# Turning the new query and key vectors at the end of an attention step, and splitting them one step later

## What is computed

```
h = rms_norm(x) ;  q, k, v, gates = split(h @ w_in)
q, k = rms_norm of each head's 64 columns
y_a = block-sparse attention (8 heads) ;  y_b = three-branch attention (8 heads)
x = x + (sigmoid(g_a) * (y_a @ w_br_moba) + sigmoid(g_b) * (y_b @ w_br_nsa)) @ w_o
u = causal conv3(rms_norm(x) @ w_up) ;  x = x + (gelu(u_a) * u_b) @ w_down
x = x + sigmoid(x @ w_ple_gate) * (p @ w_ple)
```

## The kernel before

| steps | vectors turned | beside them on PE |
|---|---|---|
| 4-7, 12-15, 20-23 | units 2, 3, 4 | projection of the next unit, 5, 6, 5, 5 rows; tiles 6 and 7 are split in the first of these steps, and used in the second |
| 28-31 | unit 5 | nothing |
| 43-46 | unit 6 | unit 7's projection, 2 rows a step, and a gate piece |
| 62-65 | unit 7 | a gate piece |

## Time and profile before

### The profile page before, as it was taken

One profiled execution on the slowest core, in us unless ns is written; L12 is line 12 of the kernel. 1 busy time (PEld: TensorE's weight loads), 2 busy tenths in 40 slices (PEclk: granted clock), 3 DMA queues, 4 the chain that ended last, 5 costly groups with the idle time before them and its releaser, 6 DMA issues.

```text
span 965.8 us, 13152 instructions
## 1 busy us (share of the span) xinstructions
PE 903.8 (94%) x4585; PEld 776.9 (80%) x4585; DVE 439.6 (46%) x969; ACT 406.1 (42%) x857; POOL 407.6 (42%) x413
## 2 busy tenths in 40 slices
PE   6898899896988878989999999999999999999998
PEld 6897898895968767877778788888888888888887
DVE  6717647756474654454541454443333343021034
ACT  5222554554553545464443455444444453232231
POOL 4632423423241424255646164445544445444450
PEclk8998999997999999999999999999999999999999
DMA  5755234135002112334653154333333333332313
GB/s 164 164 138 140 52 88 115 34 83 125 23 23 61 39 55 73 102 132 163 210 196 117 56 188 117 99 94 92 100 107 98 99 98 98 98 98 87 98 55 131
DMA packets 101363, 99.31 MB, mean 103 GB/s; under 512 B 15956, under 2 KB 76084, under 8 KB 101300
## 3 DMA queue, kind: packets, MB, share of 16 engines
q1 hardware_dynamic: 101247, 98.48, 34.9%
q10 hardware_dynamic: 53, 0.01, 0.0%
HBM read 87.58 MB, written 10.88 MB: 102 GB/s over the span
## 4 chain that ended last, share of the span: by engine, by line
PE 77%; DVE 13%; ACT 4%; issue 4%; DMA 1%; POOL 0%; SPq 0%; ACTq 0%; DVEq 0%; POOLq 0%
PE banks L1490 23%; PE banks L1492 23%; PE banks L1491 23%; DVE plain_arena L1266 2%; PE banks L1633 2%; DVE plain_arena L1238 2%; DVE split_arena L1154 1%; ACT split_arena L896 1%; PE banks L1544 1%; DVE split_arena L1301 1%; PE banks L1613 1%; ACT plain_arena L871 1%; PE banks L1612 1%; PE banks L1570 1%; DMA plain_arena<-in_x_dram 1%
## 5 line engine op out<-in xcount | busy, mean ns | idle before, releaser
L1490 PE MATMUL banks<-split_arena 128*128 128x512 f32 (+4 forms) x1228 | 468.7, 382 | 9.7 <-DVE split_arena L1170 6.1
L1491 PE MATMUL banks<-split_arena 128*128 128x512 f32 (+4 forms) x1228 | 457.7, 373 | 0.0
L1492 PE MATMUL banks<-split_arena 128*128 128x512 f32 (+4 forms) x1228 | 457.6, 373 | 0.0
L692 POOL TENSOR_TENSOR split_arena<-plain_arena,split_arena 128x512 fp32r<-128x512 f32 x184 | 241.1, 1323 | 256.4 <-ACT split_arena L912 237.1
L1490 PEld LDWEIGHTS banks<-split_arena 128*128 128x128 f32 x1228 | 234.2, 191 | 47.2 <-DVE split_arena L1170 6.4
L1492 PEld LDWEIGHTS banks<-split_arena 128*128 128x128 f32 x1228 | 233.9, 190 | 35.6
L1491 PEld LDWEIGHTS banks<-split_arena 128*128 128x128 f32 x1228 | 234.6, 191 | 32.1
L912 ACT ACTIVATE split_arena<-plain_arena 128x512 fp32r<-128x512 f32 x184 | 113.0, 627 | 192.8 <-PE banks L1492 180.7
L871 ACT ACTIVATE plain_arena<-plain_arena 128x128 f32<-128x128 f32 (+1 forms) x96 | 54.0, 563 | 146.1 <-DVE plain_arena L1266 145.9
L1448 DVE SCALAR_TENSOR_TENSOR plain_arena<-banks,plain_arena 128x511 f32<-128x511 f32 x44 | 32.7, 743 | 133.2 <-ACT plain_arena L1017 133.2
L707 POOL TENSOR_SCALAR plain_arena<-plain_arena 128x128 f32<-128x128 f32 (+1 forms) x64 | 41.7, 651 | 114.8 <-DVE plain_arena L1283 114.8
(11 more groups left out here) (161 smaller groups left out, 818.4 us busy)
## 6 DMA issues: line engine op xcount, KB each, us to landing
plain_arena<-in_w_up_dram SPq DMA_DIRECT2D x88, 256.0 KB, 3.2
plain_arena<-in_w_down_dram SPq DMA_DIRECT2D x44, 256.0 KB, 2.6
plain_arena<-in_w_in_dram SPq DMA_DIRECT2D x18, 512.0 KB, 4.6
plain_arena<-in_w_in_dram SPq DMA_DIRECT2D x32, 192.0 KB, 3.6
plain_arena<-in_x_dram SPq DMA_DIRECT2D x8, 512.0 KB, 5.0
gates<-plain_arena SPq DMA_DIRECT2D x16, 256.0 KB, 2.4
plain_arena<-skew SPq DMA_DIRECT2D x16, 256.0 KB, 3.6
plain_arena<-gates SPq DMA_DIRECT2D x16, 256.0 KB, 3.7
```

The lines of the kernel that those rows point to most:

```text
L692: pool.tensor_tensor(W2l[:, c % RING, :], raw2[:, c % RING, :], W2h[:, c % RING, :].bitcast(F32), ALU.subtract).then_inc(w2_lo, 1)
L1490: nc.tensor.matmul(o, ah, bh, start=first, stop=False)
L1491: nc.tensor.matmul(o, ah, bl, start=False, stop=False)
L1492: return nc.tensor.matmul(o, al, bh, start=False, stop=last)
```

## The change

`turn_vector` moves on PE from ahead of the projection piece to the end of the step, behind the gate piece. `vec_high` and `vec_low` move from step t to step t+1: on ACT ahead of `exp(t+1)`, on DVE behind `invert(t)` and the first half of `normalise`, ahead of a gate's low copy and of `pt_low`. Nothing is added or taken away, and POOL and SP have the same list as before.

```
 ACT   for done in proj_end(t): take_proj, squares_tile ; gates
+                if t - 1 in VEC:
+                    vec_high(*VEC[t - 1])
                 if t < T:
                     exp(t)
                 if LAG <= t:
                     pt_high(t - LAG)
                 if n in range(4, NPAIR) and k == 6:
                     gather_strip(n)
-                if t in VEC:
-                    vec_high(*VEC[t])
                 if t in SPLIT:
                     w_high(*SPLIT[t])
 DVE
                 if t - 1 in NORM:
                     normalise(NORM[t - 1], 0)
+                if t - 1 in VEC:
+                    vec_low(*VEC[t - 1])
                 for j, end in gate_end.items(): (gate_low) ; pt_low ; yTl
                 for done in proj_end(t):
                     sums(*done)
-                if t in VEC:
-                    vec_low(*VEC[t])
                 if t < T:
                     if t in SPLIT:
                         w_low(*SPLIT[t])
 PE
-                if t in VEC:
-                    turn_vector(*VEC[t])
                 if t in PROJ:
                     for part in segments(t):
                         project(*part)
                 if not STEPS[t]["k"]:
                     scores(t)
                 if t in GATE:
                     gate(*GATE[t])
+                if t in VEC:
+                    turn_vector(*VEC[t])
```

## The result

| kernel | median, us | lowest to highest | runs | profiled execution | its span | mean granted clock |
|---|---|---|---|---|---|---|
| before, on the same chip | 968.81 | 965.64 to 970.72 | 16 | 967.56 | 965.8 | 0.974 |
| after | 970.80 | 968.84 to 974.15 | 16 | 973.58 | 971.8 | 0.968 |

The ratio after to before is 1.0028, with a 95% interval of 1.0015 to 1.0040: by this ratio the change costs 2.7 us (1.5 to 3.9), against +4.4 us forecast; the two medians in the table lie 2.0 us apart. The sign held, and with it the step that carried most of the sum. Two of the five terms came out with the other sign.

What follows compares the result with a forecast made beforehand. PE, busy 94% of the span, was taken as the bound, through its idle time, work after its last wait and clock. Terms 1.2 + 3.0 + 1.7 - 1.3 - 0.2 = +4.4 us on 969.73 gave 974 us, range 968.5 to 978.

Steps and rivals of the forecast that it cites:

- The mechanism in units 2 to 4: Steps 4-7, 12-15, 20-23: tile 7's low copy still binds PE, exposing one turn of 0.41 us each; +1.2 us together.
- rival 2: Projection covers the waits in steps 4-7, 12-15, 20-23 and tile 7 comes sooner; a gain, 963.4 us; chance 0.08.
- The prediction's second wait: Step 13: after idling 2.4 us before tile 6, PE idles 0.4 us more before tile 7.
- The clock term: Steps 4-7, 12-15, 20-23: PE's clock falls behind about 2.8 us idle, 1.0 us each (0 to 1.7); +3.0 us.
- Rival 1: The clock holds at the new idle places; order alone costs +1.4 us, 971.1 us; chance 0.22.
- Rival 3: Clock falls cost the full 1.7 us in three units and spread into step 32; +8.2, 978 us; chance 0.15.
- Unit 5: Steps 28-31: x = 1 released 2.5 us late, the chain partly catching up; +1.7 us, bounds 0 and +2.5.
- Unit 6: Steps 43-46: projection and gate pieces cover real waits, one turn becomes exposed; -1.3 us, bounds -0.85 and -1.7.
- Unit 7: Steps 62-65: nearly all gained only lengthens step 66's wait for L1170; -0.2 us, bounds -2.6 and +0.75.

Runs made afterwards that it cites:

- experiment 3: The changed kernel with ten unused-result matmuls filling PE's gap ahead of tile 6 in steps 5, 13 and 21: 968.19 us, 0.9991 of before.
- Experiment 1: The changed kernel with the weight tiles of units 3, 4 and 5 split one step sooner: 959.26 us, 0.9899 of before.
- Experiment 10: The kernel before with the change made for unit 5 alone (steps 28 to 31): 967.58 us, 0.9992 of before.
- experiment 5: The kernel before with the change for units 2, 3, 4 and 6 only, and weight tiles split one step sooner: 959.68 us, 0.9903 of before.
- experiment 8: The changed kernel with the gate's low copy ahead of the vector's low copy on DVE: 966.39 us, 0.9968 of before.
- experiment 4: The kernel before with the change made for unit 6 alone (steps 43 to 46): 962.78 us, 0.9942 of before.
- experiment 6: The kernel before with only the turns on PE moved late, the copies staying in place: 972.96 us, 1.0037 of before.
- experiment 9: The kernel before with the change for units 2, 3, 4, 6 and 7, tiles split a step sooner, gate's low copy first on DVE: 960.10 us, 0.9909 of before.
- experiment 2: The kernel before, without the change, with weight tiles split one step sooner: 970.12 us, 1.0020 of before.

## Why the prediction was right, and where it was not

**The mechanism in units 2 to 4 held.** The claim was that a wait at L1544 is worth its length only if nothing holds PE right behind it, and that tile 7, landing 0.06 us before PE needed it, does. Tile 7 landed at the same time to 0.01 us, and experiment 3 measured 0.42 us a unit against 0.41. Experiment 1 takes away the tile's wait, and the loss of 5.1 us in the three units turns into a gain of 5.0: most of the 6.5 us that rival 2 hoped for was there, but only with that wait gone. Rival 2 as it stood was wrong, since POOL's chain did not move. The prediction's second wait, 0.4 us ahead of tile 7, did not show; it had added it to the idle time and not to the cost.

**The clock term was right in kind and a little small.** +3.0 us was forecast, 3.9 came (5.1 less 1.25 by experiment 3), 1.3 us a unit within the stated 0 to 1.7. Rival 1, the clock holds, fell: all three units fell, behind waits of 2.77, 2.62 and 2.64 us. Its time of 971.1 us is nearer to the measured 970.8 than the forecast's 974, but by the failures below, not by its reason. Rival 3, falls at their full price and spreading into step 32, fell as well: unit 5 ran the other way.

**Unit 5 failed: +1.7 us forecast, -1.6 came.** Two steps of its working were wrong. First, "L1154, which could start only as POOL's gate half let it (so its time stays)": with the vector's copy gone, L1154 began at 230.88, 0.02 us ahead of POOL's L672, took 0.41 us, and it was L672 that grew, to 1.52 us from the 1.27 that it took before. L1154 ended 1.15 us sooner within the step than before (231.29 less 5.68, against 226.76), and everything behind it on DVE with it. So x = 1 was 1.2 us late, not 2.5. In step 12 the same argument held, because there the L672 began 0.05 us ahead. Second, the term counted no change of clock: it forecast the turns at the low clock that the rows showed. In after the clock was full again by step 31, which gave 2.1 us. Experiment 10 has the order without that luck: +0.5 us, within the stated 0 to +2.5, and experiment 1 has +0.3.

**Unit 6 held**: -1.6 us against -1.3, near the lower bound of -1.7. By step 47, ahead of the next fall, it is -1.8 in after and in experiments 1, 3, 5 and 8. Experiments 4 and 5 showed -2.3 and -3.2 by step 52; 1.3 to 1.4 us of each is the fall around 300 us of before that they lack, so the bound left out the clock here too.

**Unit 7 failed in size and sign: -0.2 us forecast, +1.3 came.** The prediction had the right line, L1170, and the right bound: "+0.75 (x = 3's low copy wholly added)". It then valued DVE's sooner start higher than this. In fact x = 3's copy stood wholly ahead of L1170, and experiment 8 puts it at 0.9 us of wait. The rest is the clock: in after, steps 62 to 65 gain 0.8 us, and then step 66 begins 1.7 us later against step 65 than before, behind low clock (0.70 from 348 to 352 us), a fall that the kernel before does not have there. It is no accident of one execution: the same 1.7 us stand between these two steps in experiments 1, 3, 6, 8 and 9, all of which have unit 7's turns late, and not in 2, 4, 5 and 10, which do not. Which wait brings it on, no run here shows. That took the term out of its bounds, since I had priced the clock only in units 2 to 4.

**The sum** is +3.3 us in the loop (5.1 - 1.6 - 1.6 + 1.3, rounded), +2.7 us by the ratio. It came out near the forecast of +4.4 partly because unit 5's error of -3.3 us and those of the other units, +0.9, -0.3 and +1.5, offset each other.

The best versions measured, experiments 1 and 5, are 1.0% faster than before. The versions 1, 5 and 9 cannot be told apart by their times.

## What to carry to other kernels

Before a wait is counted as a gain, look for what becomes ready at the moment when PE gets past it: a producer that ends within a tenth of a microsecond of its use is the next bound, and then both have to move. When a wait of two microseconds is brought together out of shorter ones, price the clock fall behind it at each such place, not only at the first. And where two instructions of DVE and POOL begin within hundredths of a microsecond, which is first decides who is slow: such a term needs both outcomes in its bounds.

## What the runs showed of the hardware

- The clock fell behind PE waits of 2.0 us (0.76 and 0.81 in the windows of the earlier trace rows) and of 2.6 to 2.8 us (0.81 and 0.77 in step 13 of after). One such fall, at a place without slack behind it, cost 1.3 us. Filling the gap with ten matmuls (experiment 3) kept the clock at 1.00 and took 3.9 us out of the three units.
- The length of the wait does not settle whether the clock falls. Ahead of step 67 PE waits 3.56 us for L1170 in before and in experiment 4; behind it the clock is 0.57 from 356 to 360 us in before, and 1.00 from 352 to 360 in experiment 4. With 3.12 us it fell in experiment 9 and not in experiment 8.
- A fall need not last equally long behind the same wait: with 4.70 us of idle in both, the clock was full again at the scores 3.8 us later in after, and still low at those 3.9 us later in experiment 10. The difference was 2.1 us for equal instructions. Experiment 4 shows the same from the other side: up to step 43 it is the kernel before, and is there 1.3 us late. So one profiled execution of this kernel tells the effect of an edit behind a fall only to about 1 to 2 us.
- A subtraction of DVE and one of POOL that read only SBUF do not run side by side. Which one waits is a matter of hundredths of a microsecond: L1154 took 1.63 us when L672 was 0.05 us ahead, and 0.41 us (for 256 columns) when it was 0.02 us ahead of L672, which then took 1.52 instead of 1.27. The Trainium skill says this in "SBUF — State Buffer", section "SBUF: two separate sides", as an exclusive lock on a shared pair of ports. The trace agrees: in both orders the one that began second is the one that grew, by 0.95 and 0.25 us. L1249, which reads a PSUM bank, ran beside L672 in its usual 0.76 us (225.42 in before).
